# The recurrence of a hybrid layer: four channel tiles one at a time, or in two pairs

## What is computed

```python
def rglru_mixer(gate_in, x_in, conv_w, conv_b, wa, ba, wx, bx, lam):
    gate = jax.nn.gelu(gate_in)
    xc = causal_depthwise_conv(x_in, conv_w, conv_b)
    xb = xc.reshape(b, s, LRU_BLOCKS, LRU_BLOCK_W)
    r = jax.nn.sigmoid(einsum('bsnc,ncd->bsnd', xb, wa).reshape(b, s, LRU_WIDTH) + ba)
    i = jax.nn.sigmoid(einsum('bsnc,ncd->bsnd', xb, wx).reshape(b, s, LRU_WIDTH) + bx)
    log_a = -LRU_C * r * jax.nn.softplus(-lam)
    a = jnp.exp(log_a)
    u = jnp.sqrt(-jnp.expm1(2.0 * log_a)) * (i * xc)
    # h[t] = a[t] * h[t-1] + u[t]
    _, h = lax.associative_scan(combine, (a, u), axis=1)
    return h * gate
```

## Time and profile before

| | |
|---|---|
| median of three runs | 3339.02 us (3338.54 to 3339.96) |
| profiled execution, whole | 3339.03 us |
| its span in the trace | 3337.2 us |
| granted clock of TensorE, mean | 0.991 |
| PE busy | 3249.3 us, 97% |
| DVE busy | 1762.3 us, 53% |
| ACT busy | 1278.4 us, 38% |

### The profile page before, as it was taken

How to read it: one execution, slowest core, us unless ns; L and a number is a source line. 1 busy time by engine, 2 the same in 40 slices (tenths; PEclk the granted TensorE clock), 3 DMA queues, 4 the chain that set the end, 5 groups by cost and what they waited for, 6 DMA issues and landing times.

```text
span 3337.2 us, 37187 instructions
## 1 busy us (share of the span) xinstructions
PE 3249.3 (97%) x14858; PEld 2600.3 (78%) x14858; DVE 1762.3 (53%) x2894; ACT 1278.4 (38%) x1949; POOL 28.8 (1%) x57
## 2 busy tenths in 40 slices
PE   7999999999999999999999999999999988999997
PEld 6888877677788888888877677878888766878886
DVE  6333688645463335433477764455334667873333
ACT  4222456534342234322355553343223455343232
POOL 0000000000000000000000000000000100000000
PEclk9999999999999999999999999999999998999999
DMA  4333322222233333333232222323333533233332
GB/s 134 101 95 95 95 82 64 73 89 77 94 94 96 100 93 92 101 98 98 91 91 71 61 83 81 96 89 101 99 97 89 104 64 63 67 88 97 97 94 73
DMA packets 282077, 297.75 MB, mean 89 GB/s; under 512 B 9776, under 2 KB 270256, under 8 KB 281904
## 3 DMA queue, kind: packets, MB, share of 16 engines
q1 hardware_dynamic: 277408, 283.15, 29.6%
q0 software_dynamic: 3536, 10.55, 1.0%
q10 hardware_dynamic: 960, 1.67, 0.1%
HBM read 293.24 MB, written 2.10 MB: 88 GB/s over the span
## 4 chain that ended last, share of the span: by engine, by line
PE 85%; DVE 9%; ACT 4%; issue 1%; DMA 1%; DVEq 0%; SPq 0%; ACTq 0%
PE bank L218 84%; DVE k_sc L180 2%; ACT k_sc L214 2%; DVE k_wl L170 1%; DVE k_sc L170 1%; PE bank L224 1%; ACT L208 1%; ACT k_wh L214 1%; DMA k_raw<-in_ffn_w_gate 0%; DVE k_sc L196 0%; DVE k_sc L184 0%; DVE k_x L180 0%; DVE k_sm L175 0%; ACT k_sc L213 0%; DVE k_xc L180 0%
## 5 line engine op out<-in xcount | busy, mean ns | idle before, releaser
L170 DVE TENSOR_TENSOR k_wl<-k_raw,k_wh 128x1024 fp32r<-128x1024 f32 x545 | 654.4, 1204 | 1133.8 <-ACT k_wh L214 1132.2
L218 PE MATMUL bank<-k_xh,k_wh 128*128 128x512 f32 x2376 | 958.3, 403 | 15.7 <-ACT k_wh L214 11.9
L218 PE MATMUL bank<-k_xl,k_wh 128*128 128x512 f32 x2376 | 929.1, 391 | 1.6 <-DVE k_xl L170 1.6
L218 PE MATMUL bank<-k_xh,k_wl 128*128 128x512 f32 x2376 | 929.5, 391 | 1.0 <-DVE k_wl L170 0.8
L214 ACT ACTIVATE k_wh<-k_raw 128x1024 fp32r<-128x1024 f32 x545 | 563.1, 1038 | 949.8 <-PE bank L218 685.0
L218 PEld LDWEIGHTS bank<-k_xh,k_wh 128*128 128x128 f32 x2376 | 448.3, 189 | 128.3 <-issue 18.2
L218 PEld LDWEIGHTS bank<-k_xl,k_wh 128*128 128x128 f32 x2376 | 448.3, 189 | 99.0 <-issue 8.7
L218 PEld LDWEIGHTS bank<-k_xh,k_wl 128*128 128x128 f32 x2376 | 447.7, 188 | 98.2 <-DVE k_wl L170 3.3
L218 PE MATMUL bank<-k_uh,k_wh 128*128 128x512 f32 x512 | 206.5, 403 | 20.5 <-ACT k_uh L214 20.5
L218 PE MATMUL bank<-k_Ga,k_wh 128*128 128x512 f32 x704 | 218.2, 391 | 0.0
L218 PE MATMUL bank<-k_Gb,k_wh 128*128 128x512 f32 x704 | 218.2, 391 | 0.0
(11 more groups left out here) (320 smaller groups left out, 3671.1 us busy)
## 6 DMA issues: line engine op xcount, KB each, us to landing
k_raw<-in_w_in SPq DMA_DIRECT2D x153, 512.0 KB, 3.7
k_raw<-in_ffn_w_gate SPq DMA_DIRECT2D x88, 512.0 KB, 3.8
k_raw<-in_ffn_w_up SPq DMA_DIRECT2D x88, 512.0 KB, 3.7
k_raw<-in_ffn_w_down SPq DMA_DIRECT2D x80, 512.0 KB, 3.4
k_raw<-in_w_out SPq DMA_DIRECT2D x28, 512.0 KB, 3.4
k_raw<-in_w_gate SPq DMA_DIRECT2D x22, 512.0 KB, 3.8
k_raw<-in_w_up SPq DMA_DIRECT2D x22, 512.0 KB, 3.7
k_raw<-in_w_down SPq DMA_DIRECT2D x20, 512.0 KB, 3.5
```

Of the source, the lines that this page charges most:

```text
L170: return q.op(lambda e: e.tensor_tensor(out, a, b, op), cost(out))
L218: fn = lambda e: e.matmul(out, l, r, start=start, stop=stop, skip_group_check=True)
```

## The change

`recurrence` now takes a tuple of tiles, and `recurrences` runs it for (0, 1) and then for (2, 3). A pair starts when the inputs and gates of both its tiles are there. The gate products and Sigmoids are issued for one tile and then the other; then both multiplications, both Tanh, a tick, both Exp, a tick, add-reciprocal-scale of one tile, a tick, of the other, a tick, both roots, a tick, and then product, scan, gate and split tile by tile. The empty tick between scaling and root is gone. Tiles 0 and 1 put their decay (a_) in the first and third quarter of `QS`, which held the early queries and is dead by then, in place of a scratch tile; tiles 2 and 3 take a scratch tile as before.

```diff
--- before.py
+++ after.py
@@ -1199,10 +1199,12 @@
             return
             yield
 
-        def recurrence():
-            for m in range(4):
-                while xt_[m] is None or gt[m] is None:
-                    yield
+        def recurrence(ms):
+
+            while any(xt_[m] is None or gt[m] is None for m in ms):
+                yield
+            st = {}
+            for m in ms:
                 b, fb = yield from self.bank([xt_[m]])
                 t = self.mm(fb + [xt_[m], twb], b, WB[:, m * P:(m + 1) * P], tl(XC, m), True, True, inc=True)
                 b2, fb2 = yield from self.wait_slot(self.MB)
@@ -1214,27 +1216,42 @@
                 self.MB.put(b, [tr_])
                 ti = self.ac([t2] + fi, i_, b2, ACT.Sigmoid, bias=vc("bx", m))
                 self.MB.put(b2, [ti])
-                yield
-                tx = self.tt([ti, xt_[m]], tl(XC, m), i_, tl(XC, m), ALU.mult)
-
-                h_ = i_
-                tt1 = self.ac([tr_, tnsp, tx], h_, r, ACT.Tanh, scale=q1[:, m:m + 1])
-                a_, fa = yield from self.wait_slot(self.SC)
-                ta = self.ac([tr_, tsp] + fa, a_, r, ACT.Exp, scale=sp[:, m:m + 1])
-                yield
-                t = self.ts([tt1, ta], r, h_, 1.0, None, ALU.add)
+                st[m] = (r, i_, tr_, ti)
+                yield
+            tx, tt1, ta, av_, free = {}, {}, {}, {}, {}
+            for m in ms:
+                r, i_, tr_, ti = st[m]
+                tx[m] = self.tt([ti, xt_[m]], tl(XC, m), i_, tl(XC, m), ALU.mult)
+                if m < 2:
+                    av_[m], fa = tl(QS, 2 * m), afq
+                else:
+                    av_[m], fa = yield from self.wait_slot(self.SC)
+                free[m] = fa
+            for m in ms:
+                tt1[m] = self.ac([st[m][2], tnsp, tx[m]], st[m][1], st[m][0], ACT.Tanh, scale=q1[:, m:m + 1])
+            yield
+            for m in ms:
+                ta[m] = self.ac([st[m][2], tsp] + free[m], av_[m], st[m][0], ACT.Exp, scale=sp[:, m:m + 1])
+            yield
+            th = {}
+            for m in ms:
+                r, h_ = st[m][0], st[m][1]
+                t = self.ts([tt1[m], ta[m]], r, h_, 1.0, None, ALU.add)
                 t = self.rcp([t], r, r)
-                t = self.stt([t], h_, h_, 2.0, r, ALU.mult, ALU.mult)
-                yield
-                yield
-                t = self.ac([t], h_, h_, ACT.Sqrt)
-                yield
-                xc = tl(XC, m)
-                t = self.tt([t, tx], xc, h_, xc, ALU.mult)
-                self.SC.put(i_, [t])
-                self.V.wait([ta, t])
+                th[m] = self.stt([t], h_, h_, 2.0, r, ALU.mult, ALU.mult)
+                yield
+            for m in ms:
+                h_ = st[m][1]
+                th[m] = self.ac([th[m]], h_, h_, ACT.Sqrt)
+            yield
+            for m in ms:
+                r, h_, xc, a_ = st[m][0], st[m][1], tl(XC, m), av_[m]
+                t = self.tt([th[m], tx[m]], xc, h_, xc, ALU.mult)
+                self.SC.put(h_, [t])
+                self.V.wait([ta[m], t])
                 t = self.V.op(lambda e, r=r, a_=a_, xc=xc: e.tensor_tensor_scan(r, a_, xc, 0.0, ALU.mult, ALU.add))
-                self.SC.put(a_, [t])
+                if m >= 2:
+                    self.SC.put(a_, [t])
                 t = self.tt([t, gt[m]], r, r, tl(GE, m), ALU.mult)
                 yield
                 while "u" not in sd or (m == 3 and "qk" not in sd):
@@ -1244,7 +1261,11 @@
                 self.SC.put(r, [yt[8 + m][1]])
                 yield
 
-        self.bg.append(recurrence())
+        def recurrences():
+            yield from recurrence((0, 1))
+            yield from recurrence((2, 3))
+
+        self.bg.append(recurrences())
         zt = [None] * 4
         dtt = [None]
         rT = RATES[3]
```

## The result

| kernel | median | range | profiled execution | its span |
|---|---|---|---|---|
| before | 3338.54 us (7 runs) | 3337.93 to 3340.31 | 3339.03 us | 3337.2 us |
| changed | 3327.02 us (7 runs) | 3324.57 to 3334.84 | 3327.08 us | 3325.2 us |

The ratio is 0.9966 with a 95% interval of 0.9955 to 0.9978: the changed kernel is 11.5 us faster.

A forecast was written before the change was run, and what follows sets the result against it. The prediction took the ScalarE-VectorE ping-pong in the third mixer's recurrence as the bound, no engine being full. Its terms 3.5 + 7.1 + 2.2 = 12.8 us took 3339.0 to 3326.2 us, own range 3320 to 3332, overall range 3312 to 3346.

The forecast's parts named there:

- The sum: Whole kernel: 3.5 for tiles 1 and 2, 7.1 for the later two, 2.2 for a restart, 12.8 us in all.
- What bounds the kernel: Third mixer's recurrence, 95.0 us: no engine is full; the ping-pong between ScalarE and VectorE is; ceiling about 24.5 us.
- The first pair, +3.5 us,: First two recurrence tiles: gain between -5 and +7.1 us, taken as half of the 7.1 us saved on the chain.
- the bank's 4.17 us: TensorE's wait for the second tile's second gate product, behind the first tile's reciprocal: sure to go.
- some of it must come back in the transposes: Attention beside the first two tiles: its work finds two reciprocals ahead, 9 us instead of 4.5, returning some gain.
- rival C: The first two tiles end 13 us earlier and both tail gaps close: 3316 us, chance 0.12.
- The second pair, 7.1 us: Last two recurrence tiles, attention nearly over: the whole 7.1 us of shorter chain is gained, bounds 0 to 11.9.
- one restart, 2.2: Tail: one of two half-clock TensorE restarts goes, ten to twelve matmuls x 0.20 us, bounds 0 and 4.6.
- the 22.1 us of the sum: Two tiles stepped together take 22.1 us of serial chain, against 29.2 for two in a row.
- Two thirds of a pair's 7.1 is overlap of the two engines, 2.56 is two table loads: Split of each pair's 7.1 us chain saving: ScalarE and VectorE overlapping, and two table loads leaving the chain.
- Buffers and waits at nothing: Scratch tiles fit, 4 + 5 of ten, cost 0 (carried 0 to 3 us); multiplication before slot waits, 0.
- A: The stall moves: reciprocals booked too short, TensorE work issued 5.5 us early; gain 0 to 5, say 3337 us, chance 0.20.
- B: Slower: attention's transposes wait behind two reciprocals in the first two tiles, +6.3 us there, 3349 us in all, chance 0.16.

The follow-up runs named there:

- the one-by-one run: The changed kernel's new recurrence code called for one tile after another, no pairs, against the kernel before: 3333.37 us, 5.9 under it (ratio 0.9982).

## Why the prediction was right, step by step

**The sum** was 12.8 us and the measurement 11.5, by the stretch 8.9 (10.5 without the spell). The forecast stands, but part of its precision is luck: its terms were right only together, and in the two traces 3.1 us of the 12.0 lie outside the stretch, where the prediction let nothing move by more than 2. The sum also has no term for the new order of the steps, which without any pair gave 5.9 us by the median and 2.7 (4.3) by the stretch; it gave all of it to the pairs.

**What bounds the kernel** was right: no engine is full, and the chain through ScalarE and VectorE sets the time. Taking 13.4 us of reciprocals out of a VectorE that was busy 60.88 us of 95 gave 13.5 us. And the chain became shorter by what the sum says, though not pair by pair. Before, ScalarE's part of it runs from 2732.89 to 2772.51 for tiles 0 and 1 and from 2777.53 to 2815.73 for tiles 2 and 3, which is 39.6 and 38.2 us. After the change it is 35.4 (2732.45 to 2767.86) and 28.1 (2774.95 to 2803.03). These are 4.2 and 10.1 us less, 14.3 for both, where the prediction had 7.1 twice; the stretch shows 8.9 of it (10.5). The lines before, then after:

```profile
2732.89 1.27 ACT L214 ACTIVATE k_sc<-bank,k_vec 128x512 f32<-128x512 f32 x2
...
2771.88 0.63 ACT L214 ACTIVATE k_ycat<-k_sc 128x512 fp32r<-128x512 f32 x1 [3.09 <-DVE k_sc L170]
...
2777.53 0.69 ACT L214 ACTIVATE k_sc<-bank,k_vec 128x512 f32<-128x512 f32 x1 [0.85 <-PE bank L218]
```

```profile
2732.45 1.27 ACT L214 ACTIVATE k_sc<-bank,k_vec 128x512 f32<-128x512 f32 x2
...
2767.22 0.64 ACT L214 ACTIVATE k_ycat<-k_sc 128x512 fp32r<-128x512 f32 x1 [3.34 <-DVE k_sc L170]
...
2774.95 0.69 ACT L214 ACTIVATE k_sc<-bank,k_vec 128x512 f32<-128x512 f32 x1 [2.47 <-PE bank L218]
...
2802.39 0.63 ACT L214 ACTIVATE k_ycat<-k_sc 128x512 fp32r<-128x512 f32 x1 [3.34 <-DVE k_sc L170]
```

Both lengths hold foreign work, and the one-by-one run has the 35 us of the first pair without a pair.

**The first pair, +3.5 us,** is the term that failed. On its own ground it loses 1.1 us, 2.7 with the spell. The prediction had its two parts: the bank's 4.17 us did leave (0.99 is left), and "some of it must come back in the transposes" came true, though not in the transposes: it is 4.64 us ahead of attention's last product. That product's copy stands on ScalarE behind the root that waits for the second reciprocal, so TensorE is held by the chain here, and it pays once more when it starts again: attention's 40 small products take 4.07 us where they took 2.41 (granted clock 0.52 in 2760 to 2763 us, 1.00 in the kernel before). What I took as the rest, half of the chain's 7.1, is eaten up by this. The pair's real worth, 6.3 us when alone (7.9 without the spell), is paid in the tail. The prediction had a gain in the tail through the first pair as rival C and gave it 0.12; but C's reason, an earlier end of the first pair, isn't it (50.2 and 49.5 us to the third tile's first sigmoid). It is the place of z's drain and the splits in the lists.

**The second pair, 7.1 us, and one restart, 2.2,** were 9.3 together; alone it gave 10.0 (11.6). Behind the first pair it adds only 2.6 (8.9 less 6.3), as part of that had been had already. The chain itself was longer than the 22.1 us of the sum, 28.1 us, since z's drain, two halves of a split and two late gate products stood inside it. VectorE's timeline shows the reciprocals 4.46 us apart in the first pair, as summed, and 6.78 in the second, with the foreign work between them:

```profile
2746.73 3.35 DVE L196 RECIPROCAL k_sc<-k_sc 128x512 f32<-128x512 f32 x1
...
2751.19 3.35 DVE L196 RECIPROCAL k_sc<-k_sc 128x512 f32<-128x512 f32 x1
...
2784.93 3.35 DVE L196 RECIPROCAL k_sc<-k_sc 128x512 f32<-128x512 f32 x1
...
2788.92 1.28 DVE L180 SCALAR_TENSOR_TENSOR k_z<-k_z,bank 128x512 f32<-128x512 f32 x2
2790.12 1.22 DVE L170 TENSOR_TENSOR k_wl<-k_raw,k_wh 128x1024 fp32r<-128x1024 f32 x1
...
2791.71 3.35 DVE L196 RECIPROCAL k_sc<-k_sc 128x512 f32<-128x512 f32 x1
```

**"Two thirds of a pair's 7.1 is overlap of the two engines, 2.56 is two table loads"**: the kernels without reciprocals show that what the pairs gain doesn't hang on an overlap with the reciprocals. How much of the gain is table loads on the chain, how much handovers and how much the order of the steps was not separated.

**The table loads** went from 18 to 13 (12 to 14 forecast), and the root's are worth 0.1 us of the stretch. The drain of some 1.38 us on top of a load that the Trainium skill states ("ScalarE: Activation LUTs", section "What ACT_TABLE_LOAD costs") doesn't show after the change either: the load at 2755.95 takes 1.28 us and the Gelu starts at 2757.24.

**Buffers and waits at nothing** held as far as TensorE's waits show: none of them is for a scratch tile.

**The rivals.** A was seen in small, 1.9 us at the third tile's gate product against the 3 that would have decided for it. B's mechanism is there too, 4.6 us for attention's copy where 5 would have decided; it stood on ScalarE behind the second root and not in the transposes, as I had put it. How far either grows hangs on the order of the steps: with the roots eight ticks later the first reaches 5.8 us and the second goes.

## What to carry to other kernels

Where TensorE waits now for one engine and now for another while none is full, look for one chain that hands work to and fro, and count its length; booking an operation at its true length, which moves only the places of the instructions and leaves the chain as long as it was, changed only the place where TensorE stood. Two independent chains stepped together need fewer handovers and table loads (13 for 18 here), but an instruction that waits for a long operation holds everything listed behind it: issue what doesn't depend on it first, and let it wait last. Run the new steps without the pairs as well: here they were a third to a half of the gain. And gains of two such edits in a row needn't add up, since the first also moves where the later work stands against everything else in the lists.

## What was new about the hardware

Spells at the lower clock came and went between traces in places where the instruction lists are the same. In 904 to 914 us the mean granted clock was 0.83 before and 1.00 after, with TensorE busy all of the ten microseconds in both, and the same two waits of 0.8 us each in the nine ahead of them. Of the thirteen kernels, nine have 0.83 to 0.90 there and four 1.00. Behind the first gate product of the stretch, after a wait of 2.1 to 2.3 us in all, eight lose 1.6 us at the lower clock (4.7 to 4.8 us between the first tile's two gate products) and five don't (3.15 to 3.16). What sets such a spell off was not found, and with one trace for each kernel it can't be told whether it changes from one execution to the next. Each is worth about 1.6 or 1.7 us (for the first an estimate, 10 us at 0.17 less clock), and differences of 2 to 6 us were to be told here. A length taken within one stretch leaves out the spells outside it, but not the one inside: it has to be looked for before two lengths are compared.
